# Decode attention of a hybrid decoder step: key turns by VectorE blocks and block-diagonal queries, one sample a turn, joined in two batches of four

## What is computed

```
q_lat  = einsum("bqhe,rhe->bqhr", q_nope, w_uk)          # 8 samples, 8 heads, latent 256
s_past = einsum("bqhr,bkr->bhqk", q_lat, c_past) + einsum("bqhe,bke->bhqk", q_pe, kpe_past)
s_new  = the same against the token's own latent and key
p      = softmax(concat([s_past, s_new]) * MLA_SCALE)     # 1024 past tokens + 1
o_lat  = einsum("bhqk,bkr->bqhr", p[past], c_past) + einsum("bhqk,bkr->bqhr", p[new], c_new)

mem_k  = einsum("bmd,dhe->bmhe", rms_norm(mem), w_mk)     # prompt's memory keys, 256 tokens
```

## Time and profile before

| | |
|---|---|
| time before, median of 3 runs | 1197.95 us (1197.59 to 1198.65) |
| time of the profiled execution | 1199.14 us |
| its span | 1197.5 us |
| TensorE busy | 1147.5 us, 96% |
| VectorE busy | 894.9 us, 75% |
| ScalarE busy | 643.2 us, 54% |
| decode stage of layer 0, from the first `keys` to `out_part(0, CC, KC)` | 318.38 to 404.74 us, 86.4 us |
| the same of layer 1 | 907.74 to 994.29 us, 86.6 us |

### The profile page before, as it was taken

The page is one execution under the profiler, slowest core; times in us unless marked ns, Lnnn a source line. Parts: engine busy times, 40 slices in busy tenths (PEclk is TensorE's granted clock), DMA queues, the critical chain, the costliest instruction groups (busy, mean ns, idle before and its releaser), DMA issues. The chain is left out here.

```text
span 1197.5 us, 25816 instructions
## 1 busy us (share of the span) xinstructions
PE 1147.5 (96%) x10203; PEld 1059.9 (89%) x10203; DVE 894.9 (75%) x1527; ACT 643.2 (54%) x1130; POOL 172.8 (14%) x282
## 2 busy tenths in 40 slices
PE   6999999999999999998879999999999999999988
PEld 6999999999777899987869999999986779999877
DVE  5689988889767544677587998888897674448756
ACT  7474454545457444565565645444545664446554
POOL 1210101010353000032011010101014520001310
PEclk9999999999999999999989999999999999999999
DMA  7795756475568466687447766665754765667852
GB/s 214 187 263 142 220 137 179 121 187 135 167 188 239 140 186 179 188 249 269 119 117 195 201 174 188 163 164 138 187 146 138 219 195 157 181 189 215 266 206 73
DMA packets 318971, 216.13 MB, mean 180 GB/s; under 512 B 21620, under 2 KB 300512, under 8 KB 318298
## 3 DMA queue, kind: packets, MB, share of 16 engines
q1 hardware_dynamic: 301728, 164.64, 50.1%
q0 software_dynamic: 16800, 49.83, 13.2%
q10 hardware_dynamic: 330, 0.11, 0.0%
HBM read 209.31 MB, written 7.15 MB: 181 GB/s over the span
## 5 line engine op out<-in xcount | busy, mean ns | idle before, releaser
L1329 ACT ACTIVATE whi<-stage 128x2048 fp32r<-128x2048 f32 (+2 forms) x157 | 272.9, 1739 | 277.7 <-PE U L691 233.0
L1951 DVE TENSOR_TENSOR wlo<-stage,whi 128x2048 fp32r<-128x2048 f32 x138 | 315.8, 2288 | 130.2 <-ACT whi L1329 130.1
L689 PE MATMUL U<-Ahi,whi 128*128 128x264 f32 x1152 | 333.5, 290 | 1.4 <-DVE wlo L1951 0.8
L690 PE MATMUL U<-Alo,whi 128*128 128x264 f32 x1152 | 327.0, 284 | 0.0
L691 PE MATMUL U<-Ahi,wlo 128*128 128x264 f32 x1152 | 326.5, 283 | 0.0
L689 PEld LDWEIGHTS U<-Ahi,whi 128*128 128x128 f32 x1152 | 217.3, 189 | 5.4 <-DVE wlo L1951 1.7
L690 PEld LDWEIGHTS U<-Alo,whi 128*128 128x128 f32 x1152 | 217.5, 189 | 0.0
L691 PEld LDWEIGHTS U<-Ahi,wlo 128*128 128x128 f32 x1152 | 216.4, 188 | 0.0
L2128 DVE SCALAR_TENSOR_TENSOR acc<-uext,cwall,acc 128x256 f32<-128x256 f32 x464 | 189.2, 479 | 0.4
L689 PE MATMUL U<-Bhi,whi 128*128 128x264 f32 x384 | 109.1, 284 | 0.0
L690 PE MATMUL U<-Blo,whi 128*128 128x264 f32 x384 | 108.9, 284 | 0.0
(11 more groups left out here) (460 smaller groups left out, 2171.8 us busy)
## 6 DMA issues: line engine op xcount, KB each, us to landing
stage<-in_w_in SPq DMA_DIRECT2D x76, 1024.0 KB, 6.0
stage<-in_w_out SPq DMA_DIRECT2D x32, 1024.0 KB, 5.8
stage<-in_w_mk SPq DMA_DIRECT2D x8, 1024.0 KB, 6.2
cp<-in_cache_kv_latent POOLq DMA_DIRECT2D x64, 128.0 KB, 3.1
cp<-in_cache_kv_latent SPq DMA_DIRECT2D x64, 128.0 KB, 2.9
stage<-in_w_mv SPq DMA_DIRECT2D x8, 1024.0 KB, 5.4
Kt<-in_cache_mem_k POOLq DMA_DIRECT2D x16, 512.0 KB, 6.9
stage<-in_w_xq SPq DMA_DIRECT2D x8, 1024.0 KB, 7.1
```

Source lines behind the costliest of these rows:

```text
L689: mm(bk[:, 0:cols], whi[:, s, w], hi[:, k, :], start=(k == 0), stop=False)
L690: mm(bk[:, 0:cols], whi[:, s, w], lo[:, k, :], start=False, stop=False)
L1329: return A_(out, in_, ACT.Copy, scale=scale)
L1951: ins = V.tensor_tensor(wlo[:, s, :], stage[:, s, :], whi[:, s, :].bitcast(F32), ALU.subtract)
```

## The change

The eight chunks become eight **samples**: turn s handles all 1024 past tokens of sample s.

- **Key turns.** TensorE's `keys` and the copies `kt_evac` are gone. `key_turns(s)` on VectorE turns the pages in 32x32 blocks straight from SBUF to SBUF: two transposes of 128x1024 (latents of four pages each) and one of 128x512 (rope keys). The block layout fits queries that are written block-diagonally (`QB`): `spread_queries` on TensorE and `query_blocks` on ScalarE make them once a layer in a tile that GpSimd has set to zero.
- **Scores.** `scores(s)` is 10 x 4 matmuls with 32 weight columns and 64 moving columns, all of one sample. `probs(s)` is 8 matmuls of 32 by 32, its copies (`d_probs`, four of 32 partitions) and the copy of the sums (`d_out`) are ScalarE's now. `values(s)` is 8 matmuls of 32 by 256.
- **Joins.** There is no running maximum. Each of 16 page groups keeps its own maximum and sum, and four samples are joined at once: `stats_turn`, `combine_max`, `combine_exp`, `combine_weights`, `weights_turn`, `combine_pick`, `latents`, in two batches. A sample's own token enters by `new_scores`, `own_scores`, `own_rows`.
- **Order.** TensorE computes the scores of sample s+1 ahead of the probabilities of sample s.
- **Memory keys.** The four `mk` units are no longer split: TensorE multiplies the loaded `stage` tile by whole columns `memF` in plain fp32, one matmul a step. `hi(U_MK..)` and `lo(U_MK..)` and `mem_upper`/`mem_lower` go from the stage (`mem_full` writes `memF`, half of it by each engine). The memory values still need halves: they are made from `memF` during the output projection (four copies on ScalarE, four subtractions on VectorE).
- **Loads.** Since the matmul reads `stage`, the loads of `U_MK + 2`, `U_MK + 3` and output units 0 and 1 wait for the memory key unit two before them to be **done**. Sample 2's pages no longer wait for the memory columns but for the last head. `key_turns(0)` waits for the store of `uT` (its tile lies in the place of `uT`). Eight small `dmask` loads at the start are gone.

```diff
-        elif n == 2:
-            wait_apart(eng, mn_mm.sem, mn_mm.at(l, 6))
+        elif s == 2:
+            eng.wait_ge(ql_mm.sem, ql_mm.at(l, 4))
+            wait_apart(eng, att_mm.sem, att_mm.at(l, H))
         else:
-            wait_apart(eng, do_mm.sem, do_mm.at(l, n - 2))
+            wait_apart(eng, do_mm.sem, do_mm.at(l, s - 2))
...
         def load(l, u, s, dst, src):
-            sp.wait_ge(split_hi.sem, split_hi.at(l, u - NST + 1))
-            sp.wait_ge(split_lo.sem, split_lo.at(l, u - NST + 1))
+            if U_MK <= u - NST < U_MK + 4:
+                sp.wait_ge(unit_done.sem, unit_done.at(l, u - NST + 1))
+            else:
+                sp.wait_ge(split_hi.sem, split_hi.at(l, splits(u - NST)))
+                sp.wait_ge(split_lo.sem, split_lo.at(l, splits(u - NST)))
...
             load_pages(sp, l, 0, 0)
             load_pages(sp, l, 1, 0)
+            load_pages(sp, l, 2, 0)
             load_mk(2)
-            load_pages(sp, l, 2, 0)
             load_pages(sp, l, 3, 0)
+            load_pages(sp, l, 4, 0)
             load_mk(3)
-            load_pages(sp, l, 4, 0)
             load_pages(sp, l, 5, 0)
             load_out(0)
             load_pages(sp, l, 6, 0)
+            load_pages(sp, l, 7, 0)
             load_out(1)
-            load_pages(sp, l, 7, 0)
...
+            def scores(s):
+                pe.wait_ge(kb_rdy.sem, kb_rdy.at(l, s + 1))
...
+                for k in range(RBK):
+                    for g in range(4):
+                        keys = KBL[:, 2 * g:2 * g + 2, k, :] if k < RBL else KBP[:, 2 * g:2 * g + 2, k - RBL, :]
+                        last = mm(score_bank(s)[32 * g:32 * g + 32, 0:64], QB[:, s, k, :], keys, start=(k == 0), stop=(k == RBK - 1))
...
+                for k in range(k0, k0 + 4):
+                    last = mm(bk[:, 0:NM], stage[:, s % 2, k * P:(k + 1) * P], memF[:, k, 0:NM],
+                              start=(k == 0), stop=(k == KC - 1))
...
+            scores(0)
+            mks(0, 2)
+            scores(1)
             probs(0)
+            mks(2, 4)
             values(0)
+            scores(2)
+            probs(1)
+            mks(4, 5)
             pe.wait_ge(mean_rdy.sem, mean_rdy.at(l, 1))
+            squares_sum(0)
+            squares_sum(1)
+            mks(5, 6)
+            combine(5, 4)
+            values(1)
+            scores(3)
+            probs(2)
+            mks(6, 9)
+            values(2)
+            scores(4)
+            probs(3)
+            mks(9, 12)
+            stats_turn(0)
+            values(3)
+            scores(5)
+            probs(4)
+            mks(12, 15)
+            values(4)
+            scores(6)
+            probs(5)
+            weights_turn(0)
+            mks(15, 16)
+            latents(0)
+            values(5)
+            scores(7)
+            probs(6)
+            out_part(0, 0, 5)
+            own_rows()
+            values(6)
+            probs(7)
+            stats_turn(1)
+            out_part(0, 5, CC)
+            values(7)
             out_part(1, 0, 3)
+            weights_turn(1)
             out_part(1, 3, 5)
+            latents(1)
...
+            def key_turns(s):
+                if s == 0:
+                    dve.wait_ge(st_conv, l * 32 + 32)
+                for hf in range(2):
+                    dve.wait_ge(cp_load[hf][s % 3], 128 * (l * (3, 3, 2)[s % 3] + s // 3 + 1))
+                    if s and hf == 0:
+                        dve.wait_ge(ds_mm.sem, ds_mm.at(l, s))
+                    g = slice(4 * hf, 4 * hf + 4)
+                    V.transpose(KBL[:, g, :, :].rearrange("p g k a -> p (g k a)"), rawc[s % 3][:, g, :].rearrange("p g r -> p (g r)"))
+                V.transpose(KBP[:, :, :, :].rearrange("p g k a -> p (g k a)"), rawk[s % 3][:, :, :].rearrange("p g r -> p (g r)")
+                            ).then_inc(kb_rdy.sem, 1)
...
             mem_full(1)
             key_turns(0)
             mem_full(3)
             own_scores()
             mem_full(5)
             mean_off()
             mem_full(7)
             d_max(0)
             key_turns(1)
             centre()
...
             d_max(5)
             key_turns(6)
             combine_max(0)
             ln_low(2)
             ln_silu(5)
             ln_low(3)
             ln_silu(6)
             ln_low(4)
             combine_weights(0)
             combine_pick(0)
```

More of the change, by code:

```diff
@@ new lines, in probs @@
+            def probs(s):
+                pe.wait_ge(dex.sem, dex.at(l, s + 1))
+                if s >= 2:
+                    pe.wait_ge(dpT_ev.sem, dpT_ev.at(l, s - 1))
+                for t in range(2):
+                    o = 64 * (s % 2) + 32 * t
+                    for i in range(4):
+                        last = mm(HD[32 * i:32 * i + 32, o:o + 32], sD[:, s % 2, 32 * t:32 * t + 32],
+                                  ident[:, :].rearrange("p (g i h) -> p i g h", g=4, i=4)[:, i, :, :], start=True, stop=True)
+                last.then_inc(dpT_mm.sem, 1)
@@ new lines, in values @@
+            def values(s):
+                pe.wait_ge(dpT_ev.sem, dpT_ev.at(l, s + 1))
+                if s >= 2:
+                    pe.wait_ge(do_ev.sem, do_ev.at(l, s - 1))
+                o = KVL * (s % 2)
+                for t in range(2):
+                    for g in range(4):
+                        last = mm(HE[32 * g:32 * g + 32, o:o + KVL], pD[:, s % 2, t, g, :], rawc[s % 3][:, 2 * g + t, :],
+                                  start=(t == 0), stop=(t == 1))
+                last.then_inc(do_mm.sem, 1)
@@ L1047, in chunk @@
-            def chunk(n, first, second, early=lambda: None, late=lambda: None):
-                keys(n, 0)
-                keys(n, 1)
-                for i in first:
-                    mk(i)
-                early()
-                probs(n - 1)
-                keys(n, 2)
-                keys(n, 3)
-                values(n - 1)
-                keys(n, 4)
-                for i in second:
-                    mk(i)
-                late()
-                scores(n)
-            def both_squares():
-                squares_sum(0)
-                squares_sum(1)
@@ L1741, in _ @@
+            d_probs(4)
             d_exp(5)
-            kt_evac(6, 0)
-            d_alpha(5)
-            hi(U_MK + 4, 0, half=1)
-            kt_evac(6, 2)
-            ln_upper(2)
-            ln_scale(5)
-            kt_evac(6, 4)
-            ln_scale(6)
-            ln_upper(3)
+            for c in range(5, CC):
+                ln_upper(c - 3)
+                ln_scale(c)
+            combine_exp(0)
+            d_out(4)
+            d_probs(5)
             d_exp(6)
-            kt_evac(7, 0)
@@ L2398, in _ @@
-            kt_evac(2, 1)
-            d_probs(1)
-            kt_evac(2, 3)
-            lo(U_MK + 1, 1)
-            d_out(1)
-            d_max(2)
-            kt_evac(3, 1)
-            lo(U_MK + 2, 0)
-            d_probs(2)
-            kt_evac(3, 3)
-            d_out(2)
+            mem_full(1)
+            key_turns(0)
+            mem_full(3)
+            own_scores()
+            mem_full(5)
+            mean_off()
+            mem_full(7)
+            d_max(0)
+            key_turns(1)
@@ L2422, in _ @@
-            d_latent(0)
-            ln_silu(1)
-            d_probs(4)
-            kt_evac(5, 3)
+            key_turns(5)
             ln_silu(2)
-            d_out(4)
+            ln_low(0)
             ln_silu(3)
-            ln_low(0)
             ln_low(1)
+            ln_silu(4)
             d_max(5)
-            kt_evac(6, 1)
-            ln_silu(4)
-            d_probs(5)
-            kt_evac(6, 3)
-            d_out(5)
-            lo(U_MK + 4, 0)
-            d_max(6)
-            kt_evac(7, 1)
+            key_turns(6)
@@ L2440, in _ @@
+            combine_max(0)
             ln_low(2)
             ln_silu(5)
-            d_probs(6)
-            kt_evac(7, 3)
             ln_low(3)
-            d_out(6)
+            ln_silu(6)
             ln_low(4)
-            lo(U_MK + 5, 1)
-            d_max(7)
-            ln_silu(6)
-            ln_low(5)
-            ln_silu(7)
-            d_probs(7)
-            ln_low(6)
-            ln_low(7)
-            d_out(7)
-            d_norm(1)
+            combine_weights(0)
+            combine_pick(0)
@@ L2457, in _ @@
+            d_max(6)
+            key_turns(7)
+            ln_silu(7)
+            ln_low(5)
+            d_latent(0)
+            lo(U_MK + 4, 0)
+            ln_low(6)
+            d_max(7)
+            ln_low(7)
+            lo(U_MK + 5, 1)
+            combine_max(1)
+            combine_weights(1)
+            combine_pick(1)
             d_latent(1)
```

630 lines of the change are left out of this document (291 added, 339 removed).

## The result

| | before | after |
|---|---|---|
| median of the runs | 1198.3 us (4 runs, 1197.59 to 1201.01) | 1227.99 us (4 runs, 1224.24 to 1233.18) |
| ratio | | 1.0248, 95% interval 1.0224 to 1.0272 |
| profiled execution, span | 1199.14 us, 1197.5 us | 1224.24 us, 1222.6 us |
| end of the stage, layers 0 and 1 | 404.74, 994.29 us | 416.77, 1016.63 us |

The change is slower by 29.7 us by the medians, 25.1 us by the profiled executions. The forecast was 4.2 us slower with a range from 1190 to 1210 us: the sign was right, the size was outside. Of the 25.1 us, 12.0 lie in layer 0's stage, 10.3 between there and the end of layer 1's stage, and 2.8 behind it.

The account below looks back on a forecast made before the run. TensorE, busy 96% of the span, was taken as the bound. Its 12.5 us less work a layer was outweighed by waits, 2.1 us slower a layer: 1199.1 + 4.2 - 1.2 = 1202.1, said as 1202 us, range 1190 to 1210.

Parts of the forecast that it names:

- the ledger: Decode stage, turn by turn: TensorE's work plus waits, ending 2.1 us later a layer; as rival 4.2 us slower, chance 0.45.
- the allowance of 0.5 us: Layer 0's stage: 0.5 us added for changes of form on TensorE, which cost 0.1 to 0.2 us each.
- TensorE's work: Decode stage, per layer: removed and added matmul work sums to -12.5 us, about 70 us for 82.6.
- Theory C: From the experiments: TensorE's plain fp32 work is the loss; leaving pages out would gain under 10 us.
- The waits: Layer 0's decode stage: TensorE's waits sum to 21.1 us, where 3.7 us were.
- The entry: Start of layer 0's stage: key_turns(0) waits for the uT store until 321.3; scores(0) at 327.4, 3.7 us waited.
- `scores(3)` and `scores(5)`: Turns 2 and 4 of layer 0: late pages make TensorE wait 4.9 and 2.1 us.
- `lo(U_MK + 4)`: Turns 6 and 7 of layer 0: out_part(0, 0, 5) waits 1.6 us for it, behind key turn 7 on VectorE.
- Pages in time: Samples 3, 5 and 6: pages turned before TensorE asks, 9.2 us of waits a layer gone, 1184 us; chance 0.24.
- Block transposes hold up GpSimd: Page sets 4, 6 and 7 issued 2.95 us late beside key turns, 2.5 us a layer, 1207 us; chance 0.06.
- Transfers slower: Page and weight transfers at 250 GB/s for 310: 3.7 us more a layer, 1209.5 us; chance 0.12.
- A tie: Whole kernel: TensorE's gain is given back exactly, 1198 us; chance 0.13.

Follow-up runs that it names:

- the kernel with the light work apart: Changed kernel with values and pages issued earlier, earlier join, page numbers read early, both latents halved, combine_max(1) earlier: 1213.4 us, ratio 1.0130.
- both orders with the join early: Changed kernel with values(s) behind its turn's first memory-key piece, pages of 3, 5, 6 before weight tiles on SyncE, VectorE's join earlier: 1210.0 us, 1.0087.
- the one with the light work apart and the waits filled: The kernel with the light work apart, plus 6 filling matmuls ahead of scores(3) and 3 ahead of scores(5): 1210.1 us, ratio 1.0085.
- both kernels with added work: Kernel before plus, per layer, 12 matmuls of 8 moving columns (1211.0 us) or 7 of 248 (1209.0 us).
- the wide one: Kernel before plus 7 fp32 matmuls of 248 moving columns between chunk(5) and chunk(6) of each layer: 1209.0 us, ratio 1.0085.

## Why the prediction was wrong

**The step that failed** is the closing sum of the ledger: it added waits to work and priced all work at one pace. It had no term for TensorE's granted clock, which was 1.00 in every row of the stage before and fell to 0.50 behind the waits that the ledger itself forecast. In layer 0 the rows give the missing term: behind `scores(3)` 1.1 us on scores and probabilities and 0.6 on memory keys; behind `scores(5)` 1.1 and 0.5; from 385.7 to 398.3 us 1.9 on a piece, 2.1 on `latents(0)`, 0.8 on `values(5)`, 1.1 on the scores of sample 7; in the tail some 1.6 us: 10.8 us in all. 416.8 - 10.8 = 406.0 us, where the forecast said 406.9. That is 0.40 us for each of the 27.3 us at half clock, of which a part is idle. By this rate of the rows, an estimate, the 20.5 us of layer 1 and the 3.4 us near 1172 us cost 9.6 us, and 4.2 + 10.8 + 9.6 = 24.6 us, where the two profiled executions differ by 25.1. The Trainium skill, page "TensorE: Matmul & The Clock Gate", section on HAM oscillation in real kernels, describes this course (a wait for transfers, then a burst at the lower clock) and takes half of the throttled time as its cost. For 27.3 us that would be 13.7, an estimate by that page; the rows agree on the course and give 10.8.

That the rest comes within 0.9 us is in part luck. The forecast's sum says 70 us of work, but the steps of its ledger hold only 67.6 (406.4 - 317.7 us, less 21.1 of waits); with the 70 it would have ended near 409.4. Against the ledger, the stage began 0.7 us later than taken, work without the excess was 3.8 us more (71.4), waits were 4.9 us less, and the allowance of 0.5 us goes as well: 0.9 us less in all.

**TensorE's work.** Forecast 70 us for 82.6. Between 318.37 and 416.77 us TensorE is busy for 82.2 us, and without the half-clock excess for 71.4. A memory-key piece is 1.83 us for 1.72 alone or in pairs (0.46 us a matmul for 0.43) and 1.76 in threes: 1.2 us in all mis-sized. `latents` is 2.7 us at full clock for each batch, where 1.5 was taken and 2.2 was the upper bound: 2.4 us more in the two. `values` is 0.9 us for 0.98. The gain was there: the kernel with pages left out is 9 us faster than before. Theory C is refuted.

**The waits.** 16.2 us of idle time for 21.1. The entry was too dear: the store of `uT` took 2.3 us and not 4.3, VectorE began `key_turns(0)` at 320.1, and `scores(0)` came at 326.4 for 327.4, after 0.7 us of wait for 3.7 and 7.4 us of work for 6.0. `scores(3)` and `scores(5)` waited 0.7 and 1.2 us longer, `scores(6)` 1.9 us less. `lo(U_MK + 4)` cost no wait, since TensorE came later, for 1.6 us.

**The rivals.** *Pages in time* did not happen, and its price (9.2 us a layer) was too low for what it stood for: leaving these transfers out is worth 38 us, their traffic and the clock's share included. *Block transposes hold up GpSimd* is refuted: issues stay 0.59 us apart inside the key turn, so the row was right. The rule that the prediction takes from the Trainium skill, page "SBUF — State Buffer", section on who interferes with whom, speaks of VectorE's two-port modes, and this trace gives no reason to extend it to block transposes. *Transfers slower* was not the case at sample 3: the landing at 347.5 us was forecast to 0.1 us. *A tie* had no support. No rival had the clock, though the profile of before showed it: it gives the granted clock for every window, and while TensorE still had work it was below 1.00 in one place, around the layer boundary (0.63 from 594 to 608 us), where TensorE waits 9.4 us until 604.1 and its next matmuls then start 0.22 us apart for 0.12.

**What stays open.** What exactly tips the clock, and when: behind the wait of 3.1 us at `scores(5)` in layer 1 of the changed kernel it held for another 1.3 us, behind 3.3 us in layer 0 it was low at once, and behind 2.1 us at `scores(4)` in layer 0 of the kernel with the light work apart it stayed at 1.00. No complete version here beat the kernel before. The best, both orders with the join early and the one with the light work apart and the waits filled, lie 0.9% above it and take back two thirds of the loss; most of the versions between 1210 and 1213 us can't be told apart. A fourth page buffer was not tried. The 4 to 7 us by which both kernels with added work lie above their forecasts are explained in part at most: 3.5 and 6.9 us more at half clock lie outside their stages, between 420 and 906 us. In the wide one this stretch begins in a wait of 2.1 us in the cross-attention (561.0 us), where nothing had been added.

## What to carry to other kernels

When a change trades TensorE work for waits, read the granted clock by windows, and price the work behind each long wait (here 3.1 to 5.6 us) at half pace as well: here that was 20 of 25 us, by the estimate above. Where buffers come free is one chain through several queues; moving the consumer or the queue order alone only moved the wait, and both together took 15 us off. An engine's idle time may be cheaper filled than left: 22 us of useless matmuls made this kernel 10 us faster.

## What the hardware showed beyond the forecast

- The granted clock fell from 1.00 to 0.50 while TensorE was idle (0.52 from 347 to 354 us, the wait lasting until 350.5), and stayed there through dense work too: TensorE busy 12.0 of 12.0 us from 386 to 398 us at 0.50.
- At half clock scores and probabilities took 2.50 us for 1.38, a memory-key piece 3.71 for 1.83, `latents` 4.74 (389.39 to 394.13) for 2.7.
- It can also fall in light work without a wait: in 3 us of matmuls with 8 moving columns, in one of two layers of an otherwise unchanged kernel; in a wide-column control of 3.0 us in none.
- Kernels with such waits scatter more: the changed kernel 1224.2 to 1233.2 us in four runs, the kernel before 1197.6 to 1201.0. The changed kernel's two slower runs also have the lower mean clock, 0.971 and 0.970 for 0.974 and 0.976.
